# First mixer's softmax attention: probabilities divided and gated before they are turned, and the values held still with two heads side by side

## The reference, cut to what matters

```
p_c = _masked_softmax(s_c, cmp_end[None, :] <= t[:, None])      # compressed keys
o_c = p_c @ v_cmp
...
p_s = _masked_softmax(s_s, ok)                                  # selected blocks: here all causal keys
o_s = p_s @ v_g
...
p_w = _masked_softmax(s_w, ok_w)                                # window of 512: here all causal keys
o_w = p_w @ v_w
out = gn[..., 0:1] * o_c + gn[..., 1:2] * o_s + gn[..., 2:3] * o_w
```

## Time and profile before

| | |
|---|---|
| time, median of 3 runs | 2235.11 us (2228.48 to 2238.53) |
| the profiled execution: its own time, its span | 2227.64 us, 2225.8 us |
| PE busy in the span | 2133.1 us (96%) |
| PE weight loads (PEld) | 1745.6 us (78%) |
| DVE, ACT, POOL busy | 991.6, 689.6, 404.6 us |
| chain that ended last | PE 88%, ACT 4%, DVE 4%, issue 2% |
| mean granted TensorE clock | 0.982 of full speed |
| split of one tile: ACT L688, DVE L1239, mean | 1.91, 2.32 us |
| tanh L978; cast and rest of `gla` L998, L1509, mean | 0.60; 0.63, 0.68 us |
| reciprocal L1481; `n_take` L1494, L1495, mean | 0.17; 0.29, 0.29 us |

### The profile page before, as it was taken

One profiled execution on the slowest core, in us unless ns is written; L12 is line 12 of the kernel. 1 busy time (PEld: TensorE's weight loads), 2 busy tenths in 40 slices (PEclk: granted clock), 3 DMA queues, 4 the chain that ended last, 5 costly groups with the idle time before them and its releaser, 6 DMA issues.

```text
span 2225.8 us, 27541 instructions
## 1 busy us (share of the span) xinstructions
PE 2133.1 (96%) x11194; PEld 1745.6 (78%) x11194; DVE 991.6 (45%) x1386; ACT 689.6 (31%) x916; POOL 404.6 (18%) x287
## 2 busy tenths in 40 slices
PE   6998989999999899999999999899999999999998
PEld 5876768788777898878778787787777778878876
DVE  4345546826543635524834434532433444332345
ACT  5355334222221422223312212523333233212221
POOL 2000002884850201001880000200000110000000
PEclk9999899999999999999999999999999999999999
DMA  6210012553433232223453222232111222322221
GB/s 205 80 60 20 20 48 77 175 170 131 166 123 104 65 97 78 94 76 104 151 180 95 95 94 78 75 95 67 58 58 57 76 76 76 104 95 95 95 94 57
DMA packets 138984, 209.44 MB, mean 94 GB/s; under 512 B 5306, under 2 KB 114040, under 8 KB 138872
## 3 DMA queue, kind: packets, MB, share of 16 engines
q1 hardware_dynamic: 129904, 180.89, 25.2%
q0 software_dynamic: 6912, 25.17, 3.5%
q10 hardware_dynamic: 2056, 1.76, 0.3%
HBM read 205.70 MB, written 2.10 MB: 93 GB/s over the span
## 4 chain that ended last, share of the span: by engine, by line
PE 88%; ACT 4%; DVE 4%; issue 2%; POOL 1%; DMA 1%; SPq 0%; POOLq 0%; ACTq 0%; DVEq 0%
PE ps L1849 26%; PE ps L1851 25%; PE ps L1850 25%; PE ps L2245 1%; ACT w_hi L688 1%; DVE w_lo L1239 1%; PE ps L2230 1%; PE ps L1883 1%; ACT work L743 1%; PE ps L2219 1%; PE ps L2357 1%; PE ps L1889 1%; PE ps L1884 1%; PE ps L2453 1%; PE ps L2430 1%
## 5 line engine op out<-in xcount | busy, mean ns | idle before, releaser
L1239 DVE TENSOR_TENSOR w_lo<-w_raw,w_hi 128x2048 fp32r<-128x2048 f32 x163 | 377.5, 2316 | 615.4 <-ACT w_hi L688 615.3
L1849 PE MATMUL ps<-x_hi,w_hi 128*128 128x512 f32 x1280 | 517.3, 404 | 13.5 <-DVE w_lo L1239 7.6
L1850 PE MATMUL ps<-x_lo,w_hi 128*128 128x512 f32 x1280 | 507.4, 396 | 0.0
L1851 PE MATMUL ps<-x_hi,w_lo 128*128 128x512 f32 x1280 | 507.4, 396 | 0.0
L688 ACT ACTIVATE w_hi<-w_raw 128x2048 fp32r<-128x2048 f32 x164 | 313.4, 1911 | 543.1 <-PE ps L1851 436.4
L1849 PEld LDWEIGHTS ps<-x_hi,w_hi 128*128 128x128 f32 x1280 | 244.1, 191 | 78.3 <-issue 11.8
L1851 PEld LDWEIGHTS ps<-x_hi,w_lo 128*128 128x128 f32 x1280 | 242.3, 189 | 57.5
L1850 PEld LDWEIGHTS ps<-x_lo,w_hi 128*128 128x128 f32 x1280 | 242.7, 190 | 53.4 <-issue 0.5
L1849 PE MATMUL ps<-w_hi,h_hi 128*128 128x512 f32 x688 | 272.3, 396 | 7.4 <-issue 4.2
L1851 PE MATMUL ps<-w_hi,h_lo 128*128 128x512 f32 x688 | 271.5, 395 | 0.0
L1850 PE MATMUL ps<-w_lo,h_hi 128*128 128x512 f32 x688 | 271.5, 395 | 0.0
(11 more groups left out here) (336 smaller groups left out, 2720.5 us busy)
## 6 DMA issues: line engine op xcount, KB each, us to landing
w_raw<-in_ffn_w SPq DMA_DIRECT2D x64, 1024.0 KB, 5.3
ada_w<-in_w_ada POOLq DMA_DIRECT2D x48, 512.0 KB, 4.2
w_raw<-in_w_ffn_in SPq DMA_DIRECT2D x22, 1024.0 KB, 5.1
w_raw<-in_w_in SPq DMA_DIRECT2D x20, 1024.0 KB, 5.3
w_raw<-in_o_w_in SPq DMA_DIRECT2D x16, 1024.0 KB, 5.7
w_raw<-in_w_ffn_out SPq DMA_DIRECT2D x11, 1024.0 KB, 4.9
w_raw<-in_e_w_in SPq DMA_DIRECT2D x9, 1024.0 KB, 5.2
w_raw<-in_o_w_out SPq DMA_DIRECT2D x8, 1024.0 KB, 4.9
```

The lines of the kernel that those rows point to most:

```text
L1239: nc.vector.tensor_tensor(w_lo[:, slot, :], w_raw[:, slot, :], w_hi[:, slot, :].bitcast(F32), ALU.subtract).then_inc(w_lo_ready, 1)
L1849: nc.tensor.matmul(dst, a_hi, b_hi, start=start, stop=False)
L1850: nc.tensor.matmul(dst, a_hi, b_lo, start=False, stop=False)
L1851: return nc.tensor.matmul(dst, a_lo, b_hi, start=False, stop=stop_)
```

## The change

- `n_exp` also sums its row (`accum_out`), and a new step `n_scale(u)` on DVE takes the reciprocals of the two sums and multiplies `n_prob`, in place, by reciprocal and gate. The column of ones in `v_sw`, `n_norm`, `n_rows` and `n_rows_turn` are gone.
- `n_turn` has a bank for each branch (4 and 6), and `n_prob_t` has three buffers in place of two.
- `n_values(part)` now works for a pair and one branch: the values are stationary (64 columns), the turned probabilities of the two heads move (128 columns), one head's output on partitions 0 to 63 and the other's on 64 to 127 of bank 5. Both branches and the compressed one accumulate there; `n_take` reads the bank directly.
- Orders: PE issues `n_scores(u + 2)`, both turns, then `n_values` for the unit two back; ACT copies both branches and then does both exps; the splits of tiles 11 and 12 are cut in halves and spread over units 2 to 5 and 11 to 14; that of tile 13 comes behind all units. `e_out` takes its tiles in the order 2, 0, 1, 3 (`E_OUT`), so the first needs only the sparse heads 0 to 3, and the wait for `gla_ready` moves behind the first tile.

```
-        n_prob_t = place("n_prob_t", [P, 2, 2, SEQ], M_ + 8)
+        n_prob_t = [place("n_prob_t0", [P, 2, SEQ], M_ + 8), place("n_prob_t1", [P, 2, SEQ], M_ + 12),
+                    place("n_prob_t2", [P, 2, SEQ], Y_ + 56.25)]
...
+        E_OUT = (2, 0, 1, 3)
+        hi_parts = {2: (11, 0), 3: (11, 1), 11: (12, 0), 12: (12, 1)}
+        lo_parts = {4: (11, 0), 5: (11, 1), 13: (12, 0), 14: (12, 1)}
...
                 nc.scalar.activation(n_prob[:, u % 2, z, 0:nk], ps[:, 2 * (u % 2) + z, 0:nk], ACT.Exp, scale=-1.0,
-                                     bias=n_stat(u)[:, z:z + 1]).then_inc(n_exped, 1)
+                                     bias=n_stat(u)[:, z:z + 1], accum_out=n_stat(u)[:, 2 + z:3 + z]).then_inc(n_exped, 1)
...
                 act.wait_ge(n_turned, 2 * u + z + 1)
-                if u >= 2:
-                    act.wait_ge(n_valued, u - 1)
-                nc.scalar.activation(n_prob_t[:, u % 2, z, 0:nk], ps[:, 4, 0:nk], ACT.Copy).then_inc(n_copied, 1)
+                if u >= 3:
+                    act.wait_ge(n_valued, 2 * ((u - 3) // 2) + z + 1)
+                nc.scalar.activation(n_prob_t[u % 3][:, z, 0:nk], ps[:, 4 + 2 * z, 0:nk], ACT.Copy).then_inc(n_copied, 1)
...
             for u in range(N_N):
-                for z in range(2):
-                    n_copy(u, z)
-                    if u + 1 < N_N:
-                        n_exp(u + 1, z)
+                n_copy(u, 0)
+                n_copy(u, 1)
+                if u + 2 < N_N:
+                    n_exp(u + 2, 0)
+                    n_exp(u + 2, 1)
...
-            def n_norm(u):
+            def n_scale(u):
                 it, t, half = N_UNITS_E[u]
...
+                hd, nk, st_ = 2 * it + half, P * (t + 1), n_stat(u)
+                dve.wait_ge(n_exped, 2 * u + 2)
+                chain.link(nc.vector.reciprocal(st_[:, 4:6], st_[:, 2:4]))
+                for z in range(2):
+                    part = n_prob[:, u % 2, z, 0:nk]
+                    nc.vector.tensor_scalar(part, part, st_[:, 4 + z:5 + z], branch_gate[:, t, 3 * hd + 1 + z:3 * hd + 2 + z],
+                                            ALU.mult, ALU.mult).then_inc(n_scaled, 1)
...
             for u in range(N_N):
-                if u >= 2:
-                    n_norm(u - 2)
+                if u % 2 == 0 and u >= 4:
+                    n_take((u - 4) // 2)
                 if u + 2 < N_N:
                     n_max(u + 2, 0)
                     n_max(u + 2, 1)
-                if u % 2 and u >= 3:
-                    n_take((u - 3) // 2)
+                if u + 1 < N_N:
+                    n_scale(u + 1)
...
-            def n_values(u):
+            def n_values(part):
+                pair, z = divmod(part, 2)
+                it, t, half = N_UNITS_E[2 * pair]
+                g = it // 2
+                pe.wait_ge(n_copied, 2 * (2 * pair + 1) + z + 1)
+                if z == 0 and pair:
+                    pe.wait_ge(n_taken, pair)
+                for i in range(t + 1):
+                    for half in range(2):
+                        o = nc.tensor.matmul(ps[half * HD:(half + 1) * HD, 5, 0:P], v_sw[:, i, 2 * z + g, :],
+                                             n_prob_t[(2 * pair + half) % 3][:, z, i * P:(i + 1) * P],
+                                             start=(z == 0 and i == 0), stop=False)
...
             for u in range(N_N):
-                n_turn(u, 0)
                 if u + 2 < N_N:
                     n_scores(u + 2)
+                n_turn(u, 0)
                 n_turn(u, 1)
-                if u % 2 and u >= 3:
-                    n_rows_turn((u - 3) // 2)
+                if u >= 2:
+                    n_values(u - 2)
                 for x, k in r_during(u):
                     fill_r(x, k)
-                if u:
-                    n_values(u - 1)
-            pe.wait_ge(w_lo_ready, S["e_out"].first + 1)
-            pe.wait_ge(gla_ready, 4)
+            n_values(N_N - 2)
+            n_values(N_N - 1)
+            pe.wait_ge(n_taken, N_N // 4)
             e_part(0, 0)
-            n_values(N_N - 1)
             e_part(0, 1)
-            n_rows_turn(N_N // 2 - 1)
             pe.wait_ge(n_taken, N_N // 2)
             pe.wait_ge(bank_free, 4 + 2 * len(E_IN))
             e_part(0, 2)
             e_part(0, 3).then_inc(mm_done, 1)
+            pe.wait_ge(gla_ready, 4)
```

More of the change, by code:

```diff
@@ L505, in _ @@
                 load_e(i)
-            load_rows("e_out", w_eo, 0)
+            for i, chunk in enumerate(E_OUT):
+                n = S["e_out"].first + i
+                load(n, n % 2, [(by2(w_raw, n % 2), w_eo[:, 2 * chunk:2 * chunk + 2, :])])
             sp.wait_ge(n_taken, N_N // 2)
@@ L995, in _ @@
                         take_r(x)
-                for hd in {N_N - 3: (0, 1), N_N - 2: (2, 3)}.get(u, ()):
-                    act.wait_ge(gla_value, hd + 1)
-                    nc.scalar.activation(gla_hi[:, hd, :], o_gla[:, hd, :], ACT.Copy).then_inc(gla_hi_ready, 1)
+                if u in hi_parts:
+                    split_hi_part(*hi_parts[u])
+                if u == N_N - 3:
+                    gla_high(0)
+                    gla_high(1)
+            n = len(E_IN) + 1
+            split_hi(n, n % 2, loaded(n), 2 * len(E_IN))
+            gla_high(2)
+            gla_high(3)
             for i in range(1, 3):
@@ L1491, in n_take @@
                 toks = slice(t * P, (t + 1) * P)
[L1492 to L1493 removed]
+                src, hi, lo = ps[:, 5, 0:P], nsa_hi[:, it, toks], nsa_lo[:, it, toks]
+                dve.wait_ge(n_valued, 2 * pair + 2)
                 chain.link(nc.vector.tensor_copy(hi, src))
@@ L1528, in _ @@
                         gate_r(x)
[L1529 to L1532, removed]
+                if u in lo_parts:
+                    split_lo_part(*lo_parts[u])
+                if u == N_N - 2:
+                    gla_part(0)
+                    gla_part(1)
+            n_take(N_N // 2 - 2)
             n_take(N_N // 2 - 1)
+            split_lo(len(E_IN) + 1, (len(E_IN) + 1) % 2)
+            gla_part(2)
+            gla_part(3)
             for i in range(1, 3):
@@ L2223, in n_turn @@
                 it, t, half = N_UNITS_E[u]
[L2224 to L2228, removed]
+                pe.wait_ge(n_scaled, 2 * u + z + 1)
+                if u:
+                    pe.wait_ge(n_copied, 2 * (u - 1) + z + 1)
+                else:
+                    pe.wait_ge(gn_done, 2 + 2 * z)
                 for i in range(t + 1):
-                    o = nc.tensor.transpose(ps[:, 4, i * P:(i + 1) * P], n_prob[:, u % 2, z, i * P:(i + 1) * P], ident[:, :])
+                    o = nc.tensor.transpose(ps[:, 4 + 2 * z, i * P:(i + 1) * P], n_prob[:, u % 2, z, i * P:(i + 1) * P], ident[:, :])
@@ L2231, in n_turn @@
                 o.then_inc(n_turned, 1)
-            def n_values(u):
-                it, t, half = N_UNITS_E[u]
-                hd, g = 2 * it + half, it // 2
-                pe.wait_ge(n_copied, 2 * u + 2)
-                if u >= 2:
-                    pe.wait_ge(n_normed, u - 1)
-                else:
-                    pe.wait_ge(gn_done, 3 + u)
-                if half and u >= 2:
-                    pe.wait_ge(n_taken, u // 2)
-                for z in range(2):
-                    for i in range(t + 1):
-                        nc.tensor.matmul(ps[:, 5 + half, z * P:z * P + HD + 1], n_prob_t[:, u % 2, z, i * P:(i + 1) * P],
-                                         v_sw[:, i, 2 * z + g, :], start=(i == 0), stop=(i == t))
-                nc.tensor.matmul(ps[:, 5 + half, 2 * P:2 * P + HD], cmp_pt[:, hd, :], v_cmp[:, t, g, :],
-                                 start=True, stop=True).then_inc(n_valued, 1)
@@ L2250, in n_rows_turn @@
-            def n_rows_turn(pair):
-                pe.wait_ge(n_normed, 2 * pair + 2)
-                nc.tensor.transpose(ps[:, 6, 3 * P:4 * P], n_rows[:, pair % 2, :], ident[:, :]).then_inc(n_rowed, 1)
+            def n_values(part):
[10 more added lines that the diff above has]
+                                             start=(z == 0 and i == 0), stop=False)
+                for half in range(2 * z):
+                    o = nc.tensor.matmul(ps[half * HD:(half + 1) * HD, 5, 0:P], v_cmp[:, t, g, :], cmp_pt[:, 2 * it + half, :],
+                                         start=False, stop=True)
+                o.then_inc(n_valued, 1)
```

62 lines of the change are left out of this document (30 added, 32 removed).

## The result

| | before | changed |
|---|---|---|
| time, median of 4 runs each | 2234.4 us (2228.48 to 2238.53) | 2196.38 us (2195.31 to 2197.6) |
| ratio | | 0.9837 [0.9813, 0.9861] |
| profiled execution: time, span | 2227.64, 2225.8 us | 2197.6, 2195.7 us |

The change makes the kernel 1.6% faster, 38 us by these medians and 30 us between the two profiled executions. Predicted were 2198 us.

What follows compares the result with a forecast made beforehand. PE was taken to bound the attention: 178.4 + 86.9 work + 8.5 waits + 0.3 = 274.1 us to the first projection matmul, third part at 281.7, 37 us less; median 2235.11 becomes 2198 us, range 2187 to 2216.

Steps and rivals of the forecast that it cites:

- the mark: Start of the projection's third part, from which nothing waits: forecast 281.7 us against 318.63, 37 us less.
- The first projection matmul: End of the attention on PE: forecast to start at 274.1 us, against 309.48 before.
- the sum: PE's work over the 32 attention units after the change, added from turns, scores, values, form changes and fill steps: 86.9 us.
- the fill step: PE, 24 in the units: 0.78 us each before, counted at 0.70 after, without the change of form.
- Values side by side: PE's values: two heads' matmuls run beside each other, 41.6 us replaced by 28.7, 13 us less; serial rival 0.08.
- Rows no longer turned: PE in the units: the 16 turns of rows go, 2.4 us less.
- Stalls gone, clock kept: PE's two `n_rows` waits (2.8, 1.9 us) and their half clocks go; PEclk 1.00 to 270 us; clock-fall rival 0.15.
- Waits: PE's waits after the change: 1.4 us at the start, 3, 2 at units 30 and 31, 2 small; 8.5 us allowed.
- The cover of the projection's start: Tile 13's split and the `gla` casts lie under the first projection tile's four parts, 11 us; failing costs 1 or 2 us.
- Scaling: DVE in the units: 64 in-place multiplications of 0.35 us at the mean row of 320, 22.5 us.
- accumulator reads: ACT in the units: each exp also reads an accumulator, 0.194 us x 64, 12.4 us.
- Three engines this near to each other: Units: PE 86.9, ACT 81, DVE near 80 us can't all run through; rival that DVE or ACT bounds, chance 0.08.

Runs made afterwards that it cites:

- putting one stall back: Changed kernel with tile 12's split done whole behind unit 10 on ACT and DVE instead of in halves: 2202.86 us, ratio 0.9887.
- taking it out of the kernel before: Kernel before, with only tile 12's split done in halves (units 11 and 12 on ACT, 13 and 14 on DVE): 2224.34 us, ratio 0.9976.
- the kernel with one bank: Changed kernel with both branches turned in bank 4 again, the second turn waiting for the first's copy: 2223.98 us, ratio 0.9974.

## Why the prediction was right, and where it was not

- *The time*, 2198, against 2196.38: right, in part because two misses cancel. The profiled execution was to take 2191 and took 2197.6; the median was to lie 7.5 us above it and lay 1.2 below. That offset was read off three runs of before, whose later medians were 2228 to 2229: it was chance. Of the 6.6 us by which the profile was missed, 1.5 lie ahead of the first turn (179.91 us for 178.4), 0.5 up to the projection and 5.2 behind the mark, while the two parts took 0.4 less.
- *The first projection matmul* was to come 95.7 us behind the first turn and came 96.2 behind. Inside, PE's own work was 91.0 us (96.2 less 5.2 of waits) where the sum had 86.9, and the waits 5.2 where 8.5 were allowed, so these two misses cancel as well. The term that was mis-sized is the fill step, counted at 0.70 us as if it had no change of form left: it stands between 64-column values and 64-row scores and took 0.90, and 24 of them are 4.8 us more. The turns' streaming held (0.107 us a turn; the 0.16 behind a unit's turns is the change to the values, for which the sum had 0.10), and scores and values cost what they should.
- *Values side by side*, 13 us: the mechanism is shown (a key block of both heads every 0.21 us, 15 to 17 us lost without it), the size is 9.4, for the neighbours pay 3.6. The Trainium skill's rule (TensorE: Matmul & The Clock Gate, Part 3, "What overlaps and what doesn't") would have these loads exposed; two matmuls and their loads fit in 0.213 us here, so the measurement decides against it.
- *Rows no longer turned*, 2.4 us: no run prices this by itself.
- *Stalls gone, clock kept*: right; 1.00 up to 276 us. For the first stall it is shown by putting one stall back (5 to 6 us) and by taking it out of the kernel before (4 us).
- *Waits*: the start, 1.4 forecast, 0.83 measured. The end, "the copies wait behind two casts and a tanh, about 2 us", named the wrong engine: 0.73 is that, and 2.69 is DVE's take behind `gla_part`. The sum of DVE had these instructions, but at 0.68 us a `gla_lo`, and its order was not walked there.
- *The cover of the projection's start* held; the low clock cost 7.23 - 5.69 = 1.5 us for the 2 forecast.
- *What it missed altogether*: the second bank. The turns were costed "the same", which holds only with the second bank, of which the prediction doesn't speak; without it the kernel would gain 0.3%.
- *Scaling* was 26.4 us for 22.5, accumulator reads 13.5 for 12.4; neither bounds anything. "Three engines this near to each other" was too dark: with DVE's scaling or ACT's sums taken out the units lose only 1.6 and 0.6 us.
- *What follows behind the mark was said only to shift.* It grew by 5.2 us between the two profiles. At the same place of the program (PE by stretches, of before and then of the changed kernel):

```profile
741.00:755.00 14.00, 10.41 (x78) 0.88 0.25 77
```

```profile
707.00:721.00 14.00, 10.46 (x65) 0.76 0.28 84
```

From the mark to the end of the span, in windows of 1 us, 1 - PEclk adds up to 22.6 us before and 29.5 after; in the other kernels to 20.8 to 30.9, with tails of 1908.9 to 1915.1 us, the shortest tails with the smallest sums. So the tail's spread goes with the clock at waits that both kernels have. Whether the one profile of before was lucky or the shifted start makes the stretches longer, these runs don't settle. The medians of all runs, 2228.95 and 2197.08 us, lie near the two profiled times, 2227.64 and 2197.6, and are 32 us apart, not the 35.3 of the mark; that speaks for some growth behind the mark as a rule, but one more trace of the kernel before would be needed to show it.

## What to carry to other kernels

When narrow operands leave half of TensorE's columns unused, put a second independent product on the other half: here two matmuls then cost one, loads included, but the changes of form around them cost 0.1 to 0.2 us each. Two producers in a row on one engine need a buffer each, or the consumer's copy becomes the pace. On an engine that isn't the bound, look behind every long instruction for the small one that frees a bank: the take and the split both cost microseconds only by where they stood.

## What the runs showed of the hardware

- Float32 matmuls of 64 stationary and 128 moving columns on the two column halves of the array run beside each other, loads included: a pair every 0.213 us, 30.5 us busy for 192 of them, against 51.1 us with all on one half.
- Matmuls on different column halves did not keep the written order between the halves: with one head written behind the other they overlapped (units 4.9 us longer, not the 17.1 of one half), and one written later started first (189.11 us, ahead of 189.21).
- The same wait of 1.93 us was followed by 14 us of half clock in one trace and by 4 in another, and one of 1.93 us among many shorter ones, in the kernel with one bank, by none. After a fall, how long it stays down is not a constant that a sum can hold.
- The row sum of an exp on ACT is an instruction of its own, 211 ns on average. A DVE scaling in place with two per-row factors took 376 ns for 128 columns and 559 for 512: 0.48 ns a column on a base of 0.31 us.
